# VectorE and ScalarE reorder each attention step: weights, masks and exponentials first, the closings, evictions and norms of the step before behind them

## The reference

```python
for layer in range(DEPTH):                       # layers 0 and 1
    mod = cond @ w_ada[layer] + b_ada[layer]
    h = rmsnorm(x, g_pre[layer]) * (1.0 + scale) + shift
    y = even_mixer(h, ...) if layer == 0 else odd_mixer(h, ...)
    x = x + gate * rmsnorm(y, g_post[layer])
# even_mixer: mla (8 heads, causal) and swa (8 heads, window of 128), times silu(z_gate), @ w_out
# odd_mixer:  dif (4 heads, softmax(s1) - lam * softmax(s2)) and fox (8 heads, forget gate), the same
# layer 2:    cmp, sel, win (6 heads each), sb (stick-breaking, 4 heads), hgrn2 recurrence, @ w_out, layer_norm
```

## Time and profile before

| | |
|---|---|
| three runs | 1437.13, 1437.36, 1442.88 us, median 1437.36 |
| the profiled execution | 1442.61 us, its span 1441.1 us |
| PE busy | 1264.0 us, 88% |
| VectorE busy | 554.3 us, 38% |
| ScalarE busy | 427.3 us, 30% |
| mean granted clock of TensorE | 0.926 |
| attention of layers 0, 1, 2 | from 194.5 to 449, 578 to 885, 965 to 1297 us |

### The profile page before, as it was taken

One profiled execution on the slowest core, in us unless ns is written; L12 is line 12 of the kernel. 1 busy time (PEld: TensorE's weight loads), 2 busy tenths in 40 slices (PEclk: granted clock), 3 DMA queues, 4 the chain that ended last, 5 costly groups with the idle time before them and its releaser, 6 DMA issues.

```text
span 1441.1 us, 15111 instructions
## 1 busy us (share of the span) xinstructions
PE 1264.0 (88%) x5264; PEld 699.6 (49%) x5264; DVE 554.3 (38%) x1422; ACT 427.3 (30%) x1086; POOL 113.7 (8%) x140
## 2 busy tenths in 40 slices
PE   4889986899998999889999989989998999856974
PEld 1555543445564444334455555555454545545541
DVE  3233322333544520334442432112125731667871
ACT  0133022334432201322234332114233533651211
POOL 0000000000001000000000000000000000484722
PEclk9989997999998999999999999989999999966986
DMA  9222334444000432322111004241101111000000
GB/s 349 92 81 64 112 117 172 146 175 118 1 1 1 117 59 59 52 67 58 59 59 59 1 11 131 59 161 44 45 0 45 44 59 59 1 0 31 1 30 29
DMA packets 60258, 99.71 MB, mean 69 GB/s; under 512 B 12068, under 2 KB 22129, under 8 KB 60184
## 3 DMA queue, kind: packets, MB, share of 16 engines
q1 hardware_dynamic: 54370, 93.58, 20.8%
q10 hardware_dynamic: 5814, 5.18, 1.1%
HBM read 96.60 MB, written 4.08 MB: 70 GB/s over the span
## 4 chain that ended last, share of the span: by engine, by line
PE 72%; DVE 14%; ACT 5%; issue 3%; DMA 3%; POOL 2%; ACTq 1%; DVEq 0%; SPq 0%; POOLq 0%
PE PR L856 29%; PE SC L908 6%; PE OB L886 6%; PE PT L768 6%; PE PR L768 4%; PE OB L768 4%; PE SC L768 4%; PE PT L923 3%; PE PR L949 3%; DMA ring<-in_w_ada 3%; DVE d L1661 2%; DVE stage L1661 2%; POOL arena L1569 2%; DVE tok L1661 1%; DVE arena L1877 1%
## 5 line engine op out<-in xcount | busy, mean ns | idle before, releaser
L856 PE MATMUL PR<-ring,hT 128*128 128x512 f32 (+1 forms) x784 | 381.2, 599 | 9.3 <-DVE arena L1817 6.3
L1349 ACT ACTIVATE stage<-stage,nmax 128x256 f32<-128x256 f32 (+7 forms) x200 | 103.7, 519 | 335.3 <-DVE nmax L1981 311.2
L856 PEld LDWEIGHTS PR<-ring,hT 128*128 128x128 f32 x784 | 136.3, 198 | 114.4 <-issue 98.4
L886 PEld LDWEIGHTS OB<-arena,pts 128*128 128x128 f32 (+3 forms) x880 | 132.2, 202 | 97.4 <-issue 75.9
L908 PE MATMUL SC<-arena 64*128 64x256 f32 (+15 forms) x432 | 147.5, 452 | 10.0 <-DVE nmax L1981 10.0
L856 PE MATMUL PR<-hT,ring 128*128 128x512 f32 (+1 forms) x304 | 152.8, 626 | 0.0
L1569 POOL TENSOR_TENSOR arena<-arena 128x192 f32<-128x192 f32 (+1 forms) x118 | 80.5, 683 | 826.1 <-PE OB L886 778.2
L886 PE MATMUL OB<-arena,pts 128*128 128x64 f32 (+4 forms) x880 | 131.0, 278 | 9.2 <-ACT pts L1197 9.2
L923 PEld LDWEIGHTS PT<-ident,stage 128*128 128x128 f32 (+3 forms) x440 | 58.2, 145 | 131.0 <-issue 65.1
L923 PE MATMUL PT<-ident,stage 128*128 128x128 f32 (+3 forms) x440 | 87.5, 290 | 34.7 <-ACT stage L1328 15.9
L1197 ACT ACTIVATE pts<-PT 128x256 f32<-128x256 f32 (+7 forms) x200 | 80.7, 404 | 58.4 <-issue 22.2
(11 more groups left out here) (337 smaller groups left out, 1306.6 us busy)
## 6 DMA issues: line engine op xcount, KB each, us to landing
ring<-in_w_ada SPq DMA_DIRECT2D x12, 2048.0 KB, 8.8
ring<-in_od_w_in SPq DMA_DIRECT2D x8, 2048.0 KB, 14.6
ring<-in_w_in SPq DMA_DIRECT2D x5, 1536.0 KB, 6.8
ring<-in_ev_w_in SPq DMA_DIRECT2D x3, 2048.0 KB, 7.7
ring<-in_w_in SPq DMA_DIRECT2D x3, 2048.0 KB, 9.8
ring<-in_ev_w_out SPq DMA_DIRECT2D x2, 2048.0 KB, 10.1
ring<-in_od_w_out SPq DMA_DIRECT2D x2, 2048.0 KB, 8.7
ring<-in_w_out SPq DMA_DIRECT2D x2, 2048.0 KB, 7.8
```

Source lines behind the costliest of these rows:

```text
L856: mm = pe.matmul(dst, l, r, start=(k == 0), stop=(k == KT - 1))
L886: mm = pe.matmul(ob[:, h * w:h * w + w], pts[0:rows_, v % 2, n * P:n * P + P], vb, start=(n == 0), stop=(n == len(blocks) - 1))
L1349: give(act.activation(pb[:, s % NP, 0:n], zm[:, s % 2, 0:n], ACT.Exp, bias=nmax[:, row, c:c + 1], scale=-1.0, accum_out=rsum[:, row, c:c + ...
```

## The change

In each step both engines now do the previous step's left-over work one step later, behind this step's masks or exponentials. `finish_gates` and the weights of dif and cmp come first on VectorE (in step 0 the weights still behind the masks). `mT` and `hT` tiles stay in their own step. On ScalarE the left-over work stands between the exponentials and the copy of PT to `pts`. The last table line moves the tiles of dif one step forward, 15 tiles in 14 steps in place of 15.

The first `finish_behind` is ScalarE's, the second VectorE's; `finish_weights` holds the lines 1992 to 1998 as they were.

```diff
-SPREAD = [..., [(15, 15), (4, 12), (4, 8), ...
+SPREAD = [..., [(15, 14), (4, 13), (4, 8), ...
+URGENT = ("mT", "hT")
+def urgent(done):
+    return [name for name in done if name[0] in URGENT]
...
+                def finish_behind(r_, v, done):
+                    if v >= 1 and v_units[v - 1][0] == L and last_v[L, v_units[v - 1][1]] == v - 1 \
+                            and v_units[v - 1][3][0][0] == "dif":
+                        rsqrt(DH)
+                    for chain in chains:
+                        next(chain, None)
+                    for name in done:
+                        if name[0] not in URGENT:
+                            tile_done(name)
...
+                    if behind:
+                        finish_behind(*behind)
                     act.wait_ge(pt_done, v + 1)
...
                     give(copy(pts[0:r, v % 2, 0:w], PT[v % 2][0:r, 0:w]), pt_ev[v % 2], v // 2 + 1)
...
-                    for chain in chains:
-                        next(chain, None)
-                    if r_ < len(schedule[L][1]):
-                        for name in schedule[L][1][r_]:
-                            tile_done(name)
...
+                    for name in urgent(done):
+                        tile_done(name)
+                    behind = (r_, v, done)
+                finish_behind(*behind)
...
+                def finish_behind(v, done):
+                    if late_group:
+                        finish_group(*late_group.pop(), part=1)
+                    if v >= 1 and v_units[v - 1][0] == L and last_v[L, v_units[v - 1][1]] == v - 1:
+                        finish_group(L, v_units[v - 1][1])
+                    for chain in chains:
+                        next(chain, None)
+                    for name in done:
+                        if name[0] not in URGENT:
+                            tile_done(name)
...
+                    finish_gates()
+                    if r_:
+                        finish_weights(v, g, sus)
                     for s in new:
...
+                    if r_ == 0:
+                        finish_weights(v, g, sus)
+                    if behind:
+                        finish_behind(*behind)
+                    if urgent(done):
+                        finish_gates()
+                    for name in urgent(done):
+                        tile_done(name)
+                    behind = (v, done)
+                finish_gates()
+                finish_behind(*behind)
```

More of the change, by code:

```diff
@@ L152 @@
 STRIPS = 4
[L154 removed]
+SPREAD = [[(4, 5)] + [(3, 4)] * 6 + [(5, 9), (2, 1), (4, 10), (2, 1), (2, 9), (2, 5)], [(15, 14), (4, 13), (4, 8), (2, 1), (2, 5), (2, 1), (2, 1), (2, 5)], [(21, 68), (4, 14)]]
 LEFT = [(2,), (1, 2)]
 UNITS = {"adac": 1, "adas": 2, "adag": 1, "mT": 1, "hT": 1}
+URGENT = ("mT", "hT")
+def urgent(done):
+    return [name for name in done if name[0] in URGENT]
 def filler_schedule(L):
@@ L1328, in stick_tail @@
                         give(act.activation(pb[:, s % NP, 0:n], zm[:, s % 2, 0:n], ACT.Exp), p_done, s + 1)
+                def finish_behind(r_, v, done):
[7 more added lines that the diff above has]
+                            tile_done(name)
+                        if name[0] == "hf":
+                            next(chains[-1])
+                    if L == 2 and r_ in HG_EARLY:
+                        exponentials(HG_EARLY.index(r_))
+                behind = None
                 for r_, (v, (_, g, j, sus), new) in enumerate(steps(L)):
+                    done = schedule[L][1][r_] if r_ < len(schedule[L][1]) else []
                     for s in new:
@@ L1362, in attention @@
                     give(copy(pts[0:r, v % 2, 0:w], PT[v % 2][0:r, 0:w]), pt_ev[v % 2], v // 2 + 1)
-                    if v >= 1 and v_units[v - 1][0] == L and last_v[L, v_units[v - 1][1]] == v - 1 \
-                            and v_units[v - 1][3][0][0] == "dif":
-                        rsqrt(DH)
-                    for chain in chains:
-                        next(chain, None)
-                    if r_ < len(schedule[L][1]):
-                        for name in schedule[L][1][r_]:
-                            tile_done(name)
[L1371 to L1374, removed]
+                    for name in urgent(done):
+                        tile_done(name)
+                    behind = (r_, v, done)
+                finish_behind(*behind)
             def exponentials(c):
@@ L1961, in stick_tail, with finish_weights @@
                         say(stt(z, d2[:, 0:n], -1.0, z, ALU.mult, ALU.add), sb_a, "sb_a")
+                def finish_weights(v, g, sus):
+                    s = s_no[sus[-1]]
+                    n = score_operands(sus[-1])[4]
+                    row = g_no[L, g] % 16
+                    if sus[-1][0] == "dif":
+                        c = sus[0][1]
+                        dve.wait_ge(p_done, s + 1)
+                        link(dve.reciprocal(fr[:, 8:9], rsum[:, row, c + 1:c + 2]))
+                        link(stt(fr[:, 8:9], fr[:, 8:9], rsum[:, row, c:c + 1], lam[:, 5:6], ALU.mult, ALU.mult))
+                        give(stt(pb[:, s % NP, 0:n], pb[:, s % NP, 0:n], fr[:, 8:9], pb[:, (s - 1) % NP, 0:n],
+                                 ALU.mult, ALU.add), post, post_no[v] + 1)
+                    if sus[-1][0] == "cmp":
+                        dve.wait_ge(p_done, s + 1)
+                        give(tt(pb[:, s % NP, 0:n], pb[:, s % NP, 0:n], a2["cmpok"][:, plan[L][g][1], 0:n], ALU.mult),
+                             post, post_no[v] + 1)
+                def finish_behind(v, done):
[8 more added lines that the diff above has]
+                            tile_done(name)
+                behind = None
                 for r_, (v, (_, g, j, sus), new) in enumerate(steps(L)):
+                    done = schedule[L][1][r_] if r_ < len(schedule[L][1]) else []
+                    finish_gates()
+                    if r_:
+                        finish_weights(v, g, sus)
                     for s in new:
```

## The result

| | before | the change |
|---|---|---|
| median of 4 runs | 1440.12 us | 1492.52 us (1490.98 to 1495.56) |
| profiled execution, its span | 1442.61, 1441.1 | 1491.13, 1489.6 |
| PE busy | 1264.0 | 1285.9 |
| PE without an instruction | 177.1 | 203.7 |

A forecast was written before the change was run, and what follows sets the result against it. PE bounds the kernel, busy 1264.0 of 1441.1 us. Gains and new waits summed to +27 us, the clock added 8: +35 on the median 1437.36, so 1472 us, own range 1456 to 1486, overall range 1436 to 1490.

The forecast's parts named there:

- A: dif: weights ahead of the masks remove all six of PE's waits for them, −11.6 us.
- B: cmp: weights ahead of the masks remove all waits but the one behind a long reciprocal, −5.6 us.
- G: Layer 1: copies behind masks and closings make PE wait for filler banks, +22.1 us, bounds 6 and 30.
- C: Layer 0: a gate's clamp behind the next mask delays the sum tile at five steps, +7.5 us, bounds 0 and 10.
- D: Layer 0: the strips' copy behind the mask makes PE wait, +8.2 us, with +2 for the rest.
- H: fox: gate ahead of an mT tile +1.5, hT +0.9, weights of pts −0.6, together +2 us.
- I: Layer 2: a chain's reciprocal behind a mask and ahead of the closing, 2.1 us at three places, +4.3 more.
- J: End of sb: later exponentials of hgrn2 shorten PE's wait for ScalarE's stage, −2 us, bounds −6 and +2.
- K: PE's clock: new waits bring four more stretches at the lower clock, 2 us each, +8, bounds 0 and +16.
- two banks in turn hide the evictions: Faster rival, filler banks: late copies cost nothing and only the gains count, −19 us, 1418; chance 0.12.
- ScalarE's order: Slower rival, gate tiles: the copy to pts behind gate functions makes PE wait, +13 us, 1485; chance 0.15.
- The sign that I had named for it: PE's multiply into OB: waits of L886 for pts above 15 us would show the slower rival.

The follow-up runs named there:

- experiments 2 to 4: 2: kernel before, only dif/cmp weights and gate products first, 1447.61 us; 3: the change, filler tiles in own step, 1439.58; 4: 3, weights behind masks, 1443.95.
- experiments 5 and 6: 5: the change, strips and their sums in their own step, 1482.42 us; 6: the change, gates in their own step instead, 1481.91 us.
- experiment 1: The change with ScalarE's order taken back to that of the kernel before, VectorE still reordered: 1502.98 us, ratio 1.0406.
- experiment 9: The change with every filler tile in its own step, layer 2's order and the table as in the kernel before: 1431.40 us, ratio 0.9911.

## Why the prediction was right, and where it failed

**A and B (weights).** −11.6 and −5.6: the waits did go. Of the 11.6, 4.2 came back as the 5.2 at step 4 of dif, as reckoned in G. Weights ahead of the masks, the reason I gave, shorten dif by 6.0 us where they stand alone, about as much as both moves together (6.1); behind the closings' move they add 3.0 (experiments 2 to 4).

**C and D (layer 0).** The sum tiles of steps 12 to 28 wait 1.83 to 2.11 us where they waited 0.32 to 0.87, 7.2 more together where +7.5 was said; the strips' copies 1.36, 1.44 and 1.50 where 1.6 was said, and 3.05, 3.33 and 3.19 where 1.1 more than 1.91, 2.35 and 2.01 was. Right, and so is the absorbed part: the DMA wait is 6.8 instead of 9.1.

**G (layer 1).** Steps 9 to 14 wait 2.70, 3.08, 1.24, 0.52, 3.97 and 5.40 us; reckoned were 2.6, 2.9, 1.3, 0.6, 4.1 and 5.4, and 5.24 against 5.2 at step 4. Adding up what stands ahead of the release on its engine, and comparing with PE's blocks before it wants the bank, gave each within 0.2 us.

**H, I, J.** +2.8 for +2, and −3.8 for −3.3 (with B). The chains' waits of I came at the three places, 1.87, 2.48 and 3.04 us.

**K (the clock) is the step that failed**: "seven new waits of over 2 us and removes about three: four more such stretches at 2 us each, +8, bounds 0 and +16". Measured: about +22, above the upper bound. Both factors were too small. Read in slices of 1 us, the four stages have 12 stretches at the lower clock before and 19 in the change, 7 more and not 4; they last 86 us before and 149 in the change, and PE is busy in 64 and 113 of these. So 22 us for 7 stretches make 3.2 us each and not 2. The price came from one stretch of seven microseconds in part of which PE was idle; the one behind the DMA wait alone grew from 17 to 24 us. The count took 2 us as the length from which a wait matters, from one example, and so left out nearly all the waits at sum tiles and half of those at the strips. In experiments 5 and 6, where only the gates or only the strips are late, busy time of layer 0 still rises by 13.2 and 8.0 us. With 22 in K the sum is 49, which is the 48.5 between the profiled executions. The rest up to 52.4, by which the medians differ, is open. The range ended 2.5 us too low.

The Trainium skill's rule ("TensorE: Matmul & The Clock Gate", Terms), throttled time times one minus the ratio, that is, the time times what its mean clock lacks to 1, gives for layer 0 267.5 × 0.13 − 241.3 × 0.08 = 15.5 us where the busy time rose by 10.3: as in the prediction it is an upper end, since PE waits in part of that time.

**The rivals.** That two banks in turn hide the evictions (0.12) fell: waits on filler banks below 10 us were to be its sign, and they came to 35.8. For the Trainium skill's rule on rotating matmul groups through banks ("Perfetto Trace Analysis", Optimizing Tensor Performance, Matmuls) this trace adds that two banks hide no more than one tile's length: at step 13 of dif, with one block of 0.92 us left before it wanted the bank, PE waited 3.97 us. ScalarE's order (0.15) would have given 1485 and up, near the measured time, and was the wrong reason: experiment 1 is slower without it. The sign that I had named for it did come: PE waits 22.4 us for `pts`, over the 15 that I gave, where it was 9.2. Of these 16.9 lie in layer 2, 6.6 at its end, but other waits there went, and the idle time of the stage fell. So it was not a good sign.

## What to carry to other kernels

Work that gives back a buffer is worth its place by how soon the other engine wants that buffer, not by whether it looks left over: here only closings and chains, which nothing waits for within a step, could be moved behind, and only in layers 0 and 1. When two engines are nearly in step, write down for each release what stands ahead of it and what the waiter has left to do; that sum was good to 0.2 us at each of the seven sites of dif. Price the clock as its own term, with every new wait of PE and not the long ones alone, even where total idle time stays the same; and where a long wait can't be removed, filling it with a matmul that nothing reads is worth a try, ahead of the wait and not behind it.

## What the runs showed of the hardware

- Idle time of PE can stay the same (25.2 and 25.7 us in layer 0 before and in experiment 5) while the lower clock adds 13.2 us of busy time: where the waits lie counts.
- A wait of 1.82 us was followed by two slices of 4 us at a granted clock of 0.62 and 0.53, an equal one 16 us earlier by none (experiment 5). What tells the two apart stays open.
- Behind the 8.8 us DMA wait PE stayed at 0.50 from 240 to 252 us though it was busy all the time, with the strips' matmuls in it (experiment 9); with the wait filled by nine matmuls the same work ran at 1.00, and the kernel was 12 us faster than with the nine behind the wait.
